# A new order for the four token mixers, with the state-space tiles taken two at a time

## The reference, cut to what matters

```python
h = x + 0.5 * swiglu(rms_norm(x, ffn1_norm), ffn1_w_in, ffn1_w_out)
u = rms_norm(h, mix_norm)
proj = u @ w_in                     # 1024 x 6672; split into the four branches' inputs and the gates
y_sb  = stick_breaking_attention(sb_q, sb_k, sb_v)        # A, 4 heads of 64
y_s5  = s5_mixer(s5_u, lam, log_step, b, c, d, w_glu)     # B, 1024 complex states, then a GLU
y_gla = gla_mixer(gq, gk, gv, gr, gg, w_gate, ...)        # C, gated linear attention
y_dsa = dilated_mixer(d_q, d_k, d_v, ...)                 # D, windowed softmax, RoPE, query and key norms
gate = sigmoid(gates.reshape(bsz, seq, 4, 1024))
per_branch = einsum('bsnw,nwd->bsnd', branches, w_branch)
h = h + sum(gate * per_branch, axis=2) @ w_out
h = h + 0.5 * swiglu(rms_norm(h, ffn2_norm), ffn2_w_in, ffn2_w_out)
```

## Time and profile before

| | us |
|---|---|
| median of 3 runs (lowest, highest) | 1345.64 (1345.63, 1346.46) |
| the profiled execution | 1346.94 |
| its span, first to last instruction | 1345.1 |
| PE busy | 1279.2 (95%) |
| DVE busy | 907.2 (67%) |
| ACT busy | 639.4 (48%) |
| POOL busy | 362.0 (27%) |
| mean granted PE clock | 0.972 of full speed |
| read from HBM | 218.42 MB |

### The profile page before, as it was taken

The page is one execution under the profiler, slowest core; times in us unless marked ns, Lnnn a source line. Parts: engine busy times, 40 slices in busy tenths (PEclk is TensorE's granted clock), DMA queues, the critical chain, the costliest instruction groups (busy, mean ns, idle before and its releaser), DMA issues. The chain is left out here.

```text
span 1345.1 us, 25665 instructions
## 1 busy us (share of the span) xinstructions
PE 1279.2 (95%) x10328; PEld 1246.1 (93%) x10328; DVE 907.2 (67%) x1238; ACT 639.4 (48%) x876; POOL 362.0 (27%) x494
## 2 busy tenths in 40 slices
PE   5999999888999899999999999998799998999998
PEld 5999999777999799999999999997689997999998
DVE  5667767676975776555676676676878666755654
ACT  4645545552554354444455545455326443544442
POOL 0389601764000600000006893037610024000000
PEclk9999999887999899999999999998889998999999
DMA  7654554323345456555545546552223453555551
GB/s 286 220 177 166 191 184 160 123 71 109 135 157 168 146 193 220 181 176 178 183 158 191 184 156 212 172 179 94 89 101 126 163 182 126 191 195 181 183 187 64
DMA packets 31029, 220.46 MB, mean 164 GB/s; under 512 B 3568, under 2 KB 3568, under 8 KB 4592
## 3 DMA queue, kind: packets, MB, share of 16 engines
q1 hardware_dynamic: 30960, 219.49, 46.7%
HBM read 218.42 MB, written 1.05 MB: 163 GB/s over the span
## 5 line engine op out<-in xcount | busy, mean ns | idle before, releaser
L1033 DVE TENSOR_TENSOR w_lo_t<-raw,w_hi_t 128x1024 fp32r<-128x1024 f32 x408 | 516.2, 1304 | 88.2 <-ACT w_hi_t L789 88.1
L789 ACT ACTIVATE w_hi_t<-raw 128x1024 fp32r<-128x1024 f32 x408 | 408.1, 1046 | 159.9 <-PE banks L438 159.4
L436 PE MATMUL banks<-u_hi_t,w_hi_t 128*128 128x256 f32 x1552 | 450.1, 290 | 27.5 <-DVE w_lo_t L1033 14.1
L437 PE MATMUL banks<-u_lo_t,w_hi_t 128*128 128x256 f32 x1552 | 444.6, 286 | 0.0
L438 PE MATMUL banks<-u_hi_t,w_lo_t 128*128 128x256 f32 x1552 | 444.2, 286 | 0.0
L436 PEld LDWEIGHTS banks<-u_hi_t,w_hi_t 128*128 128x128 f32 x1552 | 303.7, 196 | 33.1 <-DVE u_lo_t L1433 14.4
L437 PEld LDWEIGHTS banks<-u_lo_t,w_hi_t 128*128 128x128 f32 x1552 | 303.7, 196 | 0.5 <-issue 0.5
L438 PEld LDWEIGHTS banks<-u_hi_t,w_lo_t 128*128 128x128 f32 x1552 | 303.4, 195 | 0.0
L436 PE MATMUL banks<-b_hi_t,w_hi_t 128*128 128x256 f32 x864 | 244.9, 283 | 0.0
L437 PE MATMUL banks<-b_lo_t,w_hi_t 128*128 128x256 f32 x864 | 244.6, 283 | 0.0
L438 PE MATMUL banks<-b_hi_t,w_lo_t 128*128 128x256 f32 x864 | 244.5, 283 | 0.0
(11 more groups left out here) (215 smaller groups left out, 1418.5 us busy)
## 6 DMA issues: line engine op xcount, KB each, us to landing
raw<-weights SPq DMA_DIRECT2D x203, 1024.0 KB, 4.9
prm<-params SPq DMA_DIRECT2D x1, 1178.5 KB, 5.1
prm<-params SPq DMA_DIRECT2D x1, 1166.5 KB, 15.0
cst<-constants SPq DMA_DIRECT2D x1, 1027.0 KB, 10.9
hT<-x_t SPq DMA_DIRECT2D x2, 512.0 KB, 5.5
raw<-weights SPq DMA_DIRECT2D x2, 512.0 KB, 6.3
out_t<-hT SPq DMA_DIRECT2D x4, 256.0 KB, 2.3
prm<-params SPq DMA_DIRECT2D x1, 12.0 KB, 1.7
```

The source lines that it names most:

```text
L436: pe.matmul(o, st[0], mv[0], start=start, stop=False, skip_group_check=True)
L437: pe.matmul(o, st[0], mv[1], start=False, stop=False, skip_group_check=True)
L789: act.activation(w_hi[:, slot, a:a + HALF], raw[:, slot, a:a + HALF], ACT.Copy) \
L1033: dve.tensor_tensor(w_lo[:, slot, a:a + HALF], raw[:, slot, a:a + HALF], w_hi[:, slot, a:a + HALF].bitcast(F32), ALU.subtract).then_inc(s. ...
```

## The change

All changes are in the mixer.

- `SEQ` is one list of 31 blocks: projections, gate blocks and branch blocks mixed. Gate blocks are ordered by pair of row tiles q and branch n, and the branch blocks `out0` to `out3` stand between the gate blocks (3, n). The 5 output blocks follow. The number of dense blocks is the same.
- The state-space tiles go in four pairs, after blocks 1, 4, 7 and 10 (`S5_AT`). `s5_in` and `s5_out` issue the products of both tiles in turns. `s5_rotate` is two products of 128 x 1024 and, new on DVE, an addition and a subtraction of 128 x 512; the two POOL additions are gone. The four scans of a pair run after the next block, POOL's twelve forward operations follow, and `s5_out` comes four blocks after `s5_in`.
- The pieces of the other branches are spread over later blocks, so that a step on another engine mostly has a dense block between it and the product that needs it.
- The sixteen operations of the GLA argument on DVE (L1297, L1298) are gone; ACT takes the exponential with a bias per chunk instead (16 short activations for 2 long ones), and DVE's clip is part of the product that follows. Four copies of banks by DVE go: ACT makes two, and two are read straight from the bank.
- Branch blocks use banks 4 to 7, output blocks banks 0 to 3. Output blocks 0 and 1 take row tiles 0 to 5 of both first, then 6 and 7.

```diff
-PROJ = ["s5u", "sbq", "sbk", "gg", "dq", "dk", "gqk", "sbv", "dv", "gv", "gr"]
+SEQ = ["s5u", "sbq", "sbk", "gg", "gqk", "dq", "dk", (0, 0), "sbv", "gv", (0, 1), "dv", "gr", (1, 0), (1, 1),
+       (0, 2), (0, 3), (1, 2), (1, 3), (2, 0), (2, 1), (2, 2), (2, 3),
+       (3, 0), "out0", (3, 1), "out1", (3, 2), "out2", (3, 3), "out3"]
+S5_AT = (1, 4, 7, 10)
+MIXED_AT = [((0,), (1,)), ((), ()), ((), ()), ((2, 3, 4, 5, 6), (7,))]
...
+                    def s5_in(pair):
...
                         for part in range(2):
+                            for i in (2 * pair, 2 * pair + 1):
+                                q = 32 * (i % 4)
...
+                                ins = single(banks[:, 6 + i % 2, part * T:(part + 1) * T], prm[q:q + 32, a:a + P],
+                                             s5u[q:q + 32, i // 4, :], part == 0, True)
...
                     def pieces(m):
-                        if 2 <= m < 2 + ST:
-                            s5_in(m - 2)
-                        if 5 <= m < 5 + ST:
-                            s5_out(m - 5)
+                        if m in S5_AT:
+                            s5_in(S5_AT.index(m))
+                        if m - 4 in S5_AT:
+                            s5_out(S5_AT.index(m - 4))
...
-                        if m == 5:
+                        if m == 7:
                             sb_suffix(0), sb_suffix(1)
...
-                        if m == 8:
+                        if m == 10:
                             sb_suffix(2), sb_suffix(3)
-                        if m == 10:
+                        if m == 12:
...
+                i = 2 * pair
+                bank = banks[:, 6:8, :].rearrange("p i (c t) -> p i c t", c=2)
+                wide = lambda x: x[:, i:i + 2, :].unsqueeze(2).to_broadcast([P, 2, 2, T])
+                dve.tensor_tensor(s5x[:, :, 0, :, :], bank, wide(rotC), ALU.mult)
+                dve.tensor_tensor(s5x[:, :, 1, :, :], bank, wide(rotS), ALU.mult).then_inc(s.s5_rot, 1)
+                dve.wait_ge(s.s5_rot, layer * PER.s5_rot + pair + 1)
+                re, im = s5x[:, :, 0, 0, :], s5x[:, :, 0, 1, :]
+                dve.tensor_tensor(re, re, s5x[:, :, 1, 1, :], ALU.add)
+                dve.tensor_tensor(im, im, s5x[:, :, 1, 0, :], ALU.subtract).then_inc(s.s5_x, 1)
...
+                def s5_pair(pair):
+                    pool.wait_ge(s.s5_scan, layer * PER.s5_scan + pair + 1)
+                    if pair >= 1:
+                        pool.wait_ge(s.s5_y, layer * PER.s5_y + pair)
+                    for i in range(2):
...
+                    out_part(0, range(6))
+                    block_ready(b0 + NSEQ + 1)
+                    out_part(1, range(6))
+                    out_part(0, (6, 7))
+                    out_part(1, (6, 7))
```

More of the change, by code:

```diff
@@ L164 @@
     dsa_o = 1
-    y = 4
+    y = 2
     b_hi = 4
@@ L1625, in _ @@
                 root(1)
-                for i in range(ST):
-                    s5_tile(i)
+                for pair in range(ST // 2):
+                    s5_pair(pair)
                 for dt in range(KT):
```

591 lines of the change are left out of this document (289 added, 302 removed).

## The result

The changed kernel takes 1288.86 us (median of 4 runs, 1288.52 to 1289.22), the kernel before 1345.98 (1345.63 to 1346.46): ratio 0.9575, 95% interval 0.9559 to 0.9592, 57 us less. The forecast was 1277, its range 1258 to 1306. The profiled execution took 1289.22 us, with a span of 1287.3.

A forecast was written before the change was run, and what follows sets the result against it. PE, busy 95% of the span, was taken to set the end. 46.1 + 28 + 16.3 - 20 - 2 = 68.4 us less than 1346.9 gives 1278.5; the median lies 1.3 lower: 1277 us, range 1258 to 1306.

The forecast's parts named there:

- waits, removed less new: PE's waits in both mixers: 46.1 us removed, 20 us of new waits come in their place.
- lower clock, removed less new: PE's loss at 1.2 GHz after waits in both mixers: 28 us removed, 2 us new.
- products beside each other: State-space products of two tiles overlap on PE: 16.3 us saved in both mixers, bounds 0 and 16.3.
- step 5: End of the mixer: last row tile waits 1.2 us; all new waits 10 us a mixer, lower clock after them 1.
- Step 1: Dense blocks cover PE's waits in the mixers: 46.1 us go, and 28 us at the lower clock with them.
- Step 2: State-space products issued in turns: four take the time of two (1.06 us input, 0.98 output), 16.3 us saved.
- Rival A: State-space products of a pair don't overlap on PE: 1293 us; chance 0.12.
- Step 3: Rotation, additions, exponentials and copies moved or reshaped on VectorE, POOL and ACT: 0 us on PE.
- Step 4: New PE waits in the state-space pairs, for POOL's turns of about 12.7 us, softplus and masks: 8.8 us a mixer.
- rival C: POOL's twelve operations in a row, slowed by DVE, decide: turns of 22 us, 1379 us; chance 0.04.
- Rival B: Softplus still late for the suffix sums: 13 us a mixer, 1303 us; chance 0.20.
- The signs: Trace if right: mixer idle about 10 us, PEclk 0.98 or more, four input products 1.1 us, mixer 225 to 230.

The follow-up runs named there:

- the fillers: Changed kernel with four unread products (about 1.8 us) ahead of the first and second pair's output products and the product with sbv: 1284.7 us, ratio 0.9544.

## Why the prediction was right, and where it was off

**Sign and mechanism: right.** PE's waits were the thing to win; the softplus waits are gone, those ahead of sbv fell from 5.5 and 5.7 us to 2.2, and nothing that takes their place is as long as they were. The forecast was 11.9 us low, all three of its terms too large; by its terms:

| term | forecast | measured |
|---|---|---|
| waits, removed less new | 46.1 - 20 = 26.1 | 46.7 - 22.5 = 24.2 |
| lower clock, removed less new | 28 - 2 = 26 | 28.6 - 10.1 = 18.5 |
| products beside each other | 16.3 | 13.8 |
| sum | 68.4 | 56.5 (57.7 by the executions) |

**The step that was mis-sized** is the last of step 5: "The new ones of 1 to 2.6 us lie between and far apart; the nearest row is the 0.79. I take 1 us a mixer, 2; upper bound 3.7 after each of the two longest, 15." It is 10.1, five times the value taken. The row of 0.79 us showed that the clock stayed up behind such a wait; waits of 2.0, 2.2 and 2.4 us were nearer in size to those of the old tail (2.4 and 2.7), which cost it. In the changed kernel the clock falls behind the waits of 2.0 and 1.9 us in the second mixer and not in the first, behind 2.2 in both, and not behind the one of 2.4; the fillers show that most of it hangs on the idle time.

**Step 1** holds: no suffix sum waits, and they take 2.03 us at full clock instead of 3.78. **Step 2** holds in size per piece (1.06 and 0.98) but for the wrong reason: I thought that the turns do it; it is the rows and columns. And it counted a whole piece for each one saved, 1.06 and 0.98 us, where two more products on the same rows or columns lengthen a piece by 0.86: 13.8 instead of 16.3. Above all, its gain is no gain of the kernel by itself: without it, the time is the same. The forecast kept this term apart from the waits that it lengthens and the clock behind them, so that the sum comes near is in part luck: 13.8 us of it belong to a part of the change that brings nothing here. Rival A (no overlap, 1293) had the wrong price for the same reason. **Step 3** holds where it was tested: where the additions run and how wide the rotation is are worth nothing on PE in the new order. The exponentials moved to ACT and the copies had no run of their own. In the old one the additions alone were worth 12.7 us, so the two parts of the change don't add up: each takes away the same waits.

**Step 4**, by wait (first and second mixer): the output products 2.0 and 2.0 (2.6 forecast), 2.4 and 0.7 (1.3), 0.4 and 0.3 (1.2); suffix sums 0 (1.4); sbv 2.2 and 2.2 (2.3). Together 7.0 and 5.2, forecast 8.8. DVE waits 4.4 us for POOL at the second rotation (about 5). POOL's turns were 12.7, 13.6, 13.3 and 10.7 us (12.7); the second one begins slowly, beside DVE's low part of the weights (258.56 to 260.89):

```profile
258.72 2.77 POOL L1628 TENSOR_TENSOR s5x<-s5x,G 128x256 f32<-128x256 f32 x1 [10.35 <-DVE s5x L1274]
261.44 1.09 POOL L1629 TENSOR_TENSOR s5x<-s5x,G 128x256 f32<-128x256 f32 x1
...
265.19 1.71 POOL L1634 TENSOR_TENSOR st<-s5x,st 128x256 f32<-128x256 f32 x1
...
271.55 0.72 POOL L1634 TENSOR_TENSOR st<-s5x,st 128x256 f32<-128x256 f32 x1
```

So rival C (turns of 18 us) was far off: two to four of a turn's twelve operations took about 1.6 us or more, not all. That one operation is late by 1 to 2 us and the next one is not agrees with the Trainium skill's rule (SBUF — State Buffer, Who interferes with whom).

**Step 5**: the last row tile waits 1.9 us (1.2 forecast). DVE has it at 442.99, PE goes on at 443.04, and the chain is the one forecast: gates, POOL's sum, ACT, low part. Not foreseen were 0.9 us for weights and 1.0 for the next stage's first low part behind it.

**The signs**: idle time in a mixer 11.4 and 9.2 us (about 10), PEclk 0.98 in both, four products in 1.06 us, waits of the output products 0.3 to 2.4. A mixer went from 261 and 260 to 233 and 230 us, where 225 to 230 was forecast; this is where the missing 12 us show. Rival B (softplus late) didn't happen. One sum in the prediction doesn't come out: new waits at half (10 us) and the lower clock's loss at its bound (2 x 16.7 instead of 28, 5.4 us) make 1262, not 1264, for the low end of the forecast's own range; nothing hangs on it.

## What to carry to other kernels

When the engine that sets the end is made faster, or its work packed tighter, count the waits that it runs into and the clock behind them: here 13.8 us of shorter products were worth nothing, because PE came to POOL's and DVE's results earlier, waited 8.7 us more and lost 8.7 us more to the lower clock. A wait of about 2 us is not a small thing on PE: price it with the rows of waits of its own size, and with the lower clock behind it; unread products in such a wait are a cheap way to find out what that share is, and may stay. Two parts of a change that remove the same wait must be priced together, not one after the other.

## What the runs showed of the hardware

- Small fp32 products on other rows (32 x 128) or other columns (128 x 32) of the array run beside each other in either order of issue: four in 1.07 and 0.98 us, and on the same rows or columns 1.99 and 1.91.
- The clock fell behind single waits of 1.9 to 2.4 us in some places and not in others of the same length (2.01 us at 248 us: not; at 882 us: yes); with the ones ahead of small pieces filled it stayed at 1.00 in both mixers of the profiled execution (mean clock 0.997 to 0.999 in the others). Once it fell with no wait ahead, just behind the small products, and in the other mixer of the same run it did not.
- POOL took 1.3 us for a 128 x 512 addition in the first pair of a mixer and 2.2 to 2.3 beside DVE's weights, DVE 0.69 for the same; on DVE a narrow one of 128 x 256 took 0.42 us with the rotation in narrow pieces, and 0.61 and 0.82 in the old order, where POOL was at work on other tiles.
- POOL operations of 128 x 256 took 0.73 us, and 1.7 to 2.8 where DVE made the low part of the weights.
